# Gate and up projections on one core: four low-part matmuls, then four high-part ones, per four k-blocks

## The chip, the core and the metric

The kernel runs on one core of a Trainium2 chip. The metric is the device time of one execution in microseconds (us); lower is better. Before the change it is 994.61 us, the median of three runs (993.76 to 994.87).

## What is computed

One layer of a decoder: sparse attention, a residual with a layer norm, a SwiGLU feed-forward block, and again a residual with a layer norm. There are 256 tokens of width 2048. The change touches the feed-forward block alone:

```python
D_MODEL = 2048
FFN_HIDDEN = 5632
def _swiglu(x, w_gate, w_up, w_down):
    return (jax.nn.silu(x @ w_gate) * (x @ w_up)) @ w_down
...
x = _layer_norm(DEEPNORM_ALPHA * x + m, ln1_g, ln1_b)
x = _layer_norm(DEEPNORM_ALPHA * x + _swiglu(x, w_gate, w_up, w_down), ln2_g, ln2_b)
```

All arrays are float32.

## The kernel before

**High and low parts.** The matrix engine is fed with fp32r, a reduced form of float32. To keep accuracy each factor is split in two: ScalarE copies a weight block from `raw` to `w_hi` in fp32r (L523), VectorE writes what is left over, `raw - w_hi`, to `w_lo` (L796). Activations are held the same way: `act_t[:, k, 0, :]` is the high part of k-block k (128 of the 2048 model dimensions by 256 tokens), `act_t[:, k, 1, :]` its low part. A product is then high times high, high times low, and low times high.

**Gate and up.** The hidden width of 5632 is cut into 44 column blocks of 128 (`KF`), called tiles. For one tile, gate and up each fill a PSUM bank by summing over the 16 k-blocks (`KD`). Per k-block and bank there are two matmuls. The *high part* (L1247) has the stationary operand `w_hi` and the moving operand `act_t[:, k, :, :]`, 512 columns: both parts of the activation. The *low part* (L1243) has the stationary operand `w_lo` and the moving operand `act_t[:, k, 0, :]`, 256 columns, and adds into the first half of the same bank. Each of the two has a weight load of its own. A tile is 64 matmuls: 2 banks, 16 k-blocks, a high and a low part.

**Slots.** `w_hi` and `w_lo` are rings of four slots. A slot holds eight k-blocks, so a tile takes four slots, j = 0 to 3: gate k 0 to 7, gate k 8 to 15, up the same. `ffn_tile` (L1260) waits in front of each j for VectorE's `lo_done`, calls `pairs` (L1240) for runs of two k, and behind each j raises `pe_used` (or `ffn_full` behind the last), which lets ScalarE overwrite the slot. `pairs` issues low part, low part, high part, high part for two k. For k = 0 it issues the high part first, since that matmul clears the bank. The first tile is written apart (`first_tile`, L1215, its matmuls L1221 and L1223), with 256- and 128-column matmuls for the halves of the tokens. The other 43 tiles go through `ffn_tile`: one call, then a loop of 21 turns with two tiles each.

**Around it.** SyncE issues the loads of the gate and up weights (L356, the DMA at L317), 1 MB per two slots, each waiting for `lo_done` of the block that used its place. While PE works on a tile, ScalarE and VectorE split the weights of the next one and turn the sums of the last one into `hid_t` (L582 to L590, L900 to L908). The order of each engine's program is written out by hand; semaphores join them.

**Other stages named below.** The index-query projection uses the helper `pair` (L1000 to L1004), which alternates a low and a high part per k, again with 256 and 512 columns, and with the high part first at k = 0. The down projection (`product`, L1100) is made of 512-column matmuls alone, three per k-block and token half, with `hid_t` as the stationary operand.

Of the kernel before, what the change touches and what calls it, by code (L numbers as in the profile page):

```python
# [30 lines left out]
P = 128  # L31
# [3 lines left out]
KD = D // P  # L35
# [71 lines left out]
def ring_index(v):  # L107

    x_before = sum(1 for b in X_BLOCKS for h in (0, 1) if 2 * b + h < v)
    return v - x_before  # L110


def layer_kernel(nc, a):
    ctx = ExitStack()
    with ctx:
        def sb(name, shape, dt=F32):
            return ctx.enter_context(nc.sbuf_tensor(name, shape, dt))
# [9 lines left out]
        act_t = sb("act_t", [P, KD, 2, S], F32R)  # L127
# [866 lines left out]
        def _(pe):  # L994
# [16 lines left out]
            for k, t in steps:  # L1011
                v = 2 * IN_BLOCKS[k // 2] + k % 2
                w = ring_index(v) % RING
# [3 lines left out]
                for x_part, w_part in ((0, w_hi), (0, w_lo), (1, w_hi)):  # L1017
                    for b, c0, c1 in spans:
                        last = pe.matmul(acc[:, 2 * t + b, 0:c1 - c0],  # L1019
                                         act_t[:, k, x_part, t * P:(t + 1) * P], w_part[:, w, c0:c1],  # L1020
                                         start=(k == 0 and x_part == 0 and w_part is w_hi),
                                         stop=(k == KD - 1 and x_part == 1))
# [6 lines left out]
            for t in range(TOK):  # L1029
                for n in range(KQ + KV + 1):  # L1030
                    if n == 0:
                        pe.wait_ge(proj_q_done, t + 1)
                    if n == KQ:
                        pe.wait_ge(proj_done, 2 * TOK + t + 1)
                    last = pe.transpose(tp[:, n // 2, (n % 2) * S + t * P:(n % 2) * S + (t + 1) * P],
                                        proj[:, t, n * P:(n + 1) * P], ident[:])
# [24 lines left out]
            for h in range(IDX_HEADS):  # L1061
# [4 lines left out]
                for t, c0, n in ((0, 0, P), (1, P, S)):  # L1066
                    last = pe.matmul(tp[:, h % 4, c0:c0 + n], qidx_t[rows, h // 2, t * P:(t + 1) * P],
                                     kidx_t[rows, 0:n], start=True, stop=True)
# [73 lines left out]
            for s in range(HEADS + 3):  # L1142
                if s < HEADS:
# [4 lines left out]
                    for t, c0, n in ((0, 0, P), (1, P, S)):  # L1148
                        last = pe.matmul(tp[:, s % 2, c0:c0 + n], q_t[:, g % 2, h, t * P:(t + 1) * P],  # L1149
                                         k_t[:, g % 2, h, 0:n], start=True, stop=True)  # L1150
# [5 lines left out]
                if 2 <= s < HEADS + 2:  # L1156
# [4 lines left out]
                    for n in range(KEYS // P):  # L1161
                        last = pe.transpose(tp[:, 2, n * P:(n + 1) * P], prob[:, u % 3, n * P:(n + 1) * P],  # L1162
                                            ident[:])
                    last.then_inc(pt_full, 1)
                if s >= 3:
# [3 lines left out]
                    if u >= 1:  # L1169
# [6 lines left out]
                              stop=True).then_inc(pv_full, 1)  # L1176
# [60 lines left out]
                            turn_in(1, 2 + k // 2)  # L1237
                last.then_inc(ffn_full, 1)

            def pairs(bank, w, e0, k):  # L1240

                def low_part(n):
                    pe.matmul(acc[:, bank, 0:S], w_lo[:, w, e0 + n * P:e0 + (n + 1) * P], act_t[:, k + n, 0, :],  # L1243
                              start=False, stop=False, skip_group_check=True)

                def high_part(n):
                    return pe.matmul(acc[:, bank, :], w_hi[:, w, e0 + n * P:e0 + (n + 1) * P],  # L1247
                                     act_t[:, k + n, :, :], start=(k + n == 0), stop=(k == KD - 2 and n == 0))

                if k == 0:  # L1250
                    high_part(0)
                    low_part(0)
                    low_part(1)
                    return high_part(1)
                low_part(0)
                low_part(1)
                high_part(1)
                return high_part(0)

            def ffn_tile(c, i):  # L1260
                tile = 2 * i + c
                if not (isinstance(i, int) and i == 0):
                    pe.wait_ge(ffn_comb, tile - 1)
                for j in range(4):
                    pe.wait_ge(lo_done, 2 * R_FFN + 4 * tile + j + 1)
                    for n in range(0, 8, 2):
                        k = 8 * (j % 2) + n
                        last = pairs(2 * c + j // 2, j, n * P, k)
                    last.then_inc(*((pe_used, 1) if j < 3 else (ffn_full, 1)))

            first_tile()
            ffn_tile(1, 0)
            with pe.Fori(1, KF // 2) as i:
                ffn_tile(0, i)
                ffn_tile(1, i)
# [79 lines left out]
```

## Time and profile before

| what | value |
|---|---|
| runs, median (lowest to highest) | 994.61 us (993.76 to 994.87) |
| the profiled execution's own time | 994.41 us |
| its span on the core | 992.6 us |
| mean granted TensorE clock | 0.992 of full speed |
| PE (matmul) busy | 962.3 us, 97% of the span |
| PEld (weight load) busy | 826.1 us, 83% |
| VectorE (DVE) busy | 577.9 us, 58% |
| ScalarE (ACT) busy | 522.6 us, 53% |

The profile is of one execution. PE is the matmul side of TensorE and PEld its weight-load side; they overlap. Matmuls are pipelined and the ends in their records are modelled, so two records of one engine can overlap, and what a matmul costs is read from one start to the next. In the timeline, consecutive instructions of the same kind are merged into one row, with the start of the first and a count (x2, x3). The granted clock is the share of full speed (2.4 GHz) that TensorE had; 1.00 is the 2.4 GHz level and 0.50 the 1.2 GHz level.

### The profile page before, as it was taken

What the parts mean: (1) busy time and instruction counts of PE and PEld (TensorE: products, weight loads), DVE (VectorE), ACT (ScalarE), POOL (GpSimd) and SP (SyncE); (2) the same over time, 40 slices, a digit from 0 to 9 for tenths busy, and PEclk for the clock granted to TensorE, in tenths of its full rate; (3) what the DMA queues carried; (4) which work ended last, traced back from release to release, by engine and by line L of the source; (5) the groups of instructions that cost most, each with busy time, mean ns of one, the idle gap of its engine ahead of it and who ended that gap; (6) DMA issues with size and microseconds to landing.
All of it is one profiled execution on the core that took longest, in us unless ns stands there. A gap on an engine that the chain in (4) does not pass through costs nothing.

```text
span 992.6 us, 13665 instructions
## 1 busy us (share of the span) xinstructions
PE 962.3 (97%) x5134; PEld 826.1 (83%) x5134; DVE 577.9 (58%) x787; ACT 522.6 (53%) x720; POOL 41.1 (4%) x40
## 2 busy tenths in 40 slices
PE   6988999999999999999999999999999999999995
PEld 5867888888988888888888888888888888888884
DVE  5469876568655555555555555555555454454555
ACT  5465775354455555666555555666544343343450
POOL 0003650000000000000000000000000000000000
PEclk9979999999999999999999999999999999999998
DMA  8742332566254555555555545555538465565632
GB/s 329 275 146 82 128 128 89 209 248 260 90 207 172 202 175 194 186 185 195 177 203 174 203 173 199 181 187 193 178 123 344 170 207 196 180 213 168 217 122 85
DMA packets 27117, 183.52 MB, mean 185 GB/s; under 512 B 3024, under 2 KB 3024, under 8 KB 7504
## 3 DMA queue, kind: packets, MB, share of 16 engines
q1 hardware_dynamic: 27056, 183.12, 51.9%
q8 instruction: 20, 0.33, 0.1%
q0 software_dynamic: 32, 0.00, 0.0%
q14 instruction: 9, 0.07, 0.0%
HBM read 181.01 MB, written 2.10 MB: 184 GB/s over the span
## 4 chain that ended last, share of the span: by engine, by line
PE 94%; DVE 4%; ACT 1%; issue 1%; DMA 0%; POOL 0%; DVEq 0%; ACTq 0%; POOLq 0%
PE acc L1100 33%; PE acc L1247 32%; PE acc L1243 16%; PE acc L1019 4%; PE acc L1004 1%; PE acc L1088 1%; PE acc L1221 1%; PE tp L1149 1%; PE acc L1003 1%; PE acc L1000 1%; DVE score L716 1%; PE tp L1162 0%; DVE work L746 0%; DVE w_lo L659 0%; DMA raw<-in_x_t 0%
## 5 line engine op out<-in xcount | busy, mean ns | idle before, releaser
L796 DVE TENSOR_TENSOR w_lo<-raw,w_hi 128x1024 fp32r<-128x1024 f32 (+1 forms) x286 | 340.9, 1195 | 330.5 <-ACT w_hi L523 329.5
L523 ACT ACTIVATE w_hi<-raw 128x1024 fp32r<-128x1024 f32 (+1 forms) x278 | 287.7, 1036 | 349.6 <-PE acc L1247 195.8
L1247 PE MATMUL acc<-act_t,w_hi 128*128 128x512 f32 x1376 | 432.6, 396 | 0.0
L1243 PEld LDWEIGHTS acc<-act_t,w_lo 128*128 128x128 f32 x1376 | 258.7, 188 | 57.2
L1243 PE MATMUL acc<-act_t,w_lo 128*128 128x256 f32 x1376 | 271.0, 278 | 0.0
L1247 PEld LDWEIGHTS acc<-act_t,w_hi 128*128 128x128 f32 x1376 | 216.0, 189 | 3.5
L1100 PE MATMUL acc<-w_hi,hid_t 128*128 128x512 f32 x672 | 207.3, 389 | 0.0
L1100 PEld LDWEIGHTS acc<-w_hi,hid_t 128*128 128x128 f32 x672 | 126.1, 188 | 26.1
L1100 PE MATMUL acc<-w_lo,hid_t 128*128 128x512 f32 x336 | 130.8, 389 | 0.0
L1100 PEld LDWEIGHTS acc<-w_lo,hid_t 128*128 128x128 f32 x336 | 63.1, 188 | 13.2
L1100 PE MATMUL acc<-w_hi,o_t 128*128 128x512 f32 x224 | 72.8, 397 | 0.0
L659 DVE TENSOR_TENSOR w_lo<-raw,w_hi 128x1024 fp32r<-128x1024 f32 (+1 forms) x38 | 43.1, 1144 | 18.3 <-ACT w_hi L405 18.2
L405 ACT ACTIVATE w_hi<-raw 128x1024 fp32r<-128x1024 f32 (+1 forms) x42 | 41.6, 1000 | 17.2 <-PE acc L1019 14.7
L1100 PEld LDWEIGHTS acc<-w_hi,o_t 128*128 128x128 f32 x224 | 42.1, 188 | 8.5
L1100 PE MATMUL acc<-w_lo,o_t 128*128 128x512 f32 x112 | 43.6, 390 | 0.0
L1019 PE MATMUL acc<-w_hi,act_t 128*128 128x512 f32 (+1 forms) x128 | 31.3, 366 | 9.8 <-DVE w_lo L659 9.8
L1019 PEld LDWEIGHTS acc<-w_hi,act_t 128*128 128x128 f32 x128 | 22.7, 196 | 12.8 <-DVE w_lo L659 9.8
L900 DVE TENSOR_TENSOR comb<-acc,low 128x512 f32<-128x512 f32 x44 | 30.1, 683 | 1.4 <-ACT low L582 1.4
L989 POOL TENSOR_SCALAR prob<-prob,row_inv 128x128 f32<-128x128 f32 (+1 forms) x24 | 28.8, 1213 | 21.3 <-DVE row_inv L768 21.3
L582 ACT ACTIVATE low<-acc 128x512 f32<-128x512 f32 x44 | 25.5, 580 | 4.9 <-PE acc L1223 4.9
L1004 PE MATMUL acc<-cq_t,w_hi 128*128 128x512 f32 x72 | 27.3, 407 | 0.0
L586 ACT ACT_TABLE_LOAD x21 | 26.9, 1283 | 0.4
(134 smaller groups left out, 756.7 us busy)
## 6 DMA issues: line engine op xcount, KB each, us to landing
raw<-in_w_gu SPq DMA_DIRECT2D x88, 1024.0 KB, 4.8
raw<-in_w_down SPq DMA_DIRECT2D x32, 1024.0 KB, 4.8
raw<-in_w_out SPq DMA_DIRECT2D x16, 1024.0 KB, 4.8
raw<-in_w_down SPq DMA_DIRECT2D x16, 768.0 KB, 4.2
raw<-in_w_in SPq DMA_DIRECT2D x7, 848.0 KB, 6.5
raw<-in_w_uq SPq DMA_DIRECT2D x4, 1024.0 KB, 4.8
raw<-in_w_ukv SPq DMA_DIRECT2D x4, 1024.0 KB, 4.7
ln_rows<-in_ln_rows SPq DMA_DIRECT2D x4, 1024.0 KB, 7.1
```

Of the source, the lines that this page charges most:

```text
L405: act.activation(w_hi[:, w % RING, 0:n], raw[:, r % RING, half * n:(half + 1) * n], ACT.Copy).then_inc(hi_done, 1)
L523: act.activation(w_hi[:, (2 * slot + half) % RING, 0:n], raw[:, slot, first:first + n], ACT.Copy).then_inc(hi_done, 1)
L586: act.activation(sig[:], comb[:, 0, :], ACT.Silu).then_inc(ffn_sig, 1)
L659: dve.tensor_tensor(w_lo[:, w % RING, 0:n], raw[:, r % RING, half * n:(half + 1) * n], w_hi[:, w % RING, 0:n], ALU.subtract).then_inc(lo_d ...
L796: dve.tensor_tensor(w_lo[:, h, 0:n], raw[:, slot, first:first + n], w_hi[:, h, 0:n], ALU.subtract).then_inc(lo_done, 1)
L900: dve.tensor_tensor(comb[:], acc[:, 2 * c:2 * c + 2, 0:S], low[:], ALU.add).then_inc(ffn_comb, 1)
L989: pool.tensor_scalar(prob[:, s % 3, cols], prob[:, s % 3, cols], row_inv[:, (s + 1) % 2, t:t + 1], None, ALU.mult).then_inc(prob_done, 1)
L1004: return pe.matmul(acc[:, bank, :], wh, rhs, start=False, stop=stop)
L1019: last = pe.matmul(acc[:, 2 * t + b, 0:c1 - c0], act_t[:, k, x_part, t * P:(t + 1) * P], w_part[:, w, c0:c1], start=(k == 0 and x_part == ...
L1100: last = pe.matmul(acc[:, bank0 + t, :], lhs[:, k, x, t * P:(t + 1) * P], part[:, w, n * GC:(n + 1) * GC], start=(start and x == 0 and par ...
L1243: pe.matmul(acc[:, bank, 0:S], w_lo[:, w, e0 + n * P:e0 + (n + 1) * P], act_t[:, k + n, 0, :], start=False, stop=False, skip_group_check=True)
L1247: return pe.matmul(acc[:, bank, :], w_hi[:, w, e0 + n * P:e0 + (n + 1) * P], act_t[:, k + n, :, :], start=(k + n == 0), stop=(k == KD - 2 ...
```

## The change

`pairs` becomes `fours`. For four k it issues four low parts, in rising k, and then four high parts, in falling k. For k = 0 the high part of k = 0 still comes first. `ffn_tile` calls it for n = 0 and 4 instead of n = 0, 2, 4, 6. The flag that closes a bank's sum (`stop`) moves with the last high part.

```diff
-            def pairs(bank, w, e0, k):
+            def fours(bank, w, e0, k):
 
                 def low_part(n):
                     pe.matmul(acc[:, bank, 0:S], w_lo[:, w, e0 + n * P:e0 + (n + 1) * P], act_t[:, k + n, 0, :],
...
                 def high_part(n):
                     return pe.matmul(acc[:, bank, :], w_hi[:, w, e0 + n * P:e0 + (n + 1) * P],
-                                     act_t[:, k + n, :, :], start=(k + n == 0), stop=(k == KD - 2 and n == 0))
+                                     act_t[:, k + n, :, :], start=(k + n == 0), stop=(k == KD - 4 and n == 0))
 
                 if k == 0:
                     high_part(0)
-                    low_part(0)
-                    low_part(1)
-                    return high_part(1)
-                low_part(0)
-                low_part(1)
-                high_part(1)
-                return high_part(0)
+                for n in range(4):
+                    low_part(n)
+                for n in (3, 2, 1, 0) if k > 0 else (3, 2, 1):
+                    last = high_part(n)
+                return last
...
-                    for n in range(0, 8, 2):
+                    for n in (0, 4):
                         k = 8 * (j % 2) + n
-                        last = pairs(2 * c + j // 2, j, n * P, k)
+                        last = fours(2 * c + j // 2, j, n * P, k)
```

## Rows read from the trace of the kernel before

**Rows 1.** The page: engines, chain, the two costly matmul groups, loads of gate and up.

```profile
PE 962.3 (97%) x5134; PEld 826.1 (83%) x5134; DVE 577.9 (58%) x787; ACT 522.6 (53%) x720; POOL 41.1 (4%) x40
...
PE 94%; DVE 4%; ACT 1%; issue 1%; DMA 0%; POOL 0%; DVEq 0%; ACTq 0%; POOLq 0%
PE acc L1100 33%; PE acc L1247 32%; PE acc L1243 16%; PE acc L1019 4%; PE acc L1004 1%; PE acc L1088 1%; PE acc L1221 1%; PE tp L1149 1%; PE acc L1003 1%; PE acc L1000 1%; DVE score L716 1%; PE tp L1162 0%; DVE work L746 0%; DVE w_lo L659 0%; DMA raw<-in_x_t 0%
...
L1247 PE MATMUL acc<-act_t,w_hi 128*128 128x512 f32 x1376 | 432.6, 396 | 0.0
...
L1243 PE MATMUL acc<-act_t,w_lo 128*128 128x256 f32 x1376 | 271.0, 278 | 0.0
...
raw<-in_w_gu SPq DMA_DIRECT2D x88, 1024.0 KB, 4.8
```

**Rows 2.** Busy time by stretch, gate and up stage behind its first tile.

```profile
core 0: us, PE busy (x) PEld busy (x) DVE busy (x) ACT busy (x) POOL busy (x), PEclk, DMA share, GB/s
262.80:742.40 479.60, 479.60 (x2753) 418.88 (x2753) 265.42 (x300) 282.94 (x342) 0.00 (x0) 1.00 0.53 185
```

**Rows 3.** Who waited for whom, 263 to 742 us (total, times, longest).

```profile
DVE w_lo L796 <- ACT w_hi L523: 202.7, 171, 2.7
ACT w_hi L523 <- PE acc L1247: 194.2, 130, 1.9
```

**Rows 4.** Timeline of PE: first matmul of `ffn_tile`, first of the down projection.

```profile
262.80 0.45 PE L1247 MATMUL acc<-act_t,w_hi 128*128 128x512 f32 x1
...
742.76 0.39 PE L1100 MATMUL acc<-w_hi,hid_t 128*128 128x512 f32 x1
```

**Rows 5.** Timeline of PE in the stage, 400 to 408 us.

```profile
400.29 0.40 PE L1243 MATMUL acc<-act_t,w_lo 128*128 128x256 f32 x2
400.52 0.63 PE L1247 MATMUL acc<-act_t,w_hi 128*128 128x512 f32 x2
400.99 0.39 PE L1243 MATMUL acc<-act_t,w_lo 128*128 128x256 f32 x2
...
401.92 0.86 PE L1247 MATMUL acc<-act_t,w_hi 128*128 128x512 f32 x3
402.61 0.40 PE L1243 MATMUL acc<-act_t,w_lo 128*128 128x256 f32 x2
```

**Rows 6.** Timeline of PE, index-query projection; an output begins with each row of L1000.

```profile
61.99 0.40 PE L1000 MATMUL acc<-cq_t,w_hi 128*128 128x512 f32 x1
...
63.62 0.28 PE L1001 MATMUL acc<-cq_t,w_lo 128*128 128x256 f32 x1
63.74 0.28 PE L1003 MATMUL acc<-cq_t,w_lo 128*128 128x256 f32 x1
63.87 0.40 PE L1004 MATMUL acc<-cq_t,w_hi 128*128 128x512 f32 x1
...
69.00 0.39 PE L1000 MATMUL acc<-cq_t,w_hi 128*128 128x512 f32 x1
```

**Rows 7.** Timeline of PE, two k per output; first and last of three starts.

```profile
122.68 0.39 PE L1000 MATMUL acc<-ckv_t,w_hi 128*128 128x512 f32 x1
...
124.08 0.39 PE L1000 MATMUL acc<-ckv_t,w_hi 128*128 128x512 f32 x1
```

**Rows 8.** Timeline of PE, down projection; 16 repeats of three matmuls lie between.

```profile
800.35 0.62 PE L1100 MATMUL acc<-w_hi,hid_t 128*128 128x512 f32 x2
...
811.23 0.62 PE L1100 MATMUL acc<-w_hi,hid_t 128*128 128x512 f32 x2
```

**Rows 9.** Timeline of PE in the first tile; five matmuls lie between.

```profile
246.62 0.33 PE L1221 MATMUL acc<-act_t,gu_hi 128*128 128x256 f32 x1
...
247.31 0.33 PE L1221 MATMUL acc<-act_t,gu_hi 128*128 128x256 f32 x1
```

**Rows 10.** Timeline of PE, index-query projection, two microseconds earlier.

```profile
60.59 0.42 PE L1003 MATMUL acc<-cq_t,w_lo 128*128 128x256 f32 x1
60.81 0.63 PE L1004 MATMUL acc<-cq_t,w_hi 128*128 128x512 f32 x1
61.23 0.34 PE L1003 MATMUL acc<-cq_t,w_lo 128*128 128x256 f32 x1
```

**Rows 11.** Busy time by stretch, for the granted clock (third number from the end).

```profile
57.00:61.20 4.20, 3.94 (x12) 3.44 (x13) 3.73 (x6) 2.47 (x4) 0.00 (x0) 0.50 0.02 4
61.99:69.00 7.01, 7.01 (x41) 6.12 (x40) 4.39 (x7) 4.63 (x8) 0.00 (x0) 1.00 0.44 150
```

## The prediction

> **What bounds the kernel now.** I began with the page. TensorE (PE) is busy 97% of the span, and the chain that ended last lies 94% on PE, 32% at L1247 and 16% at L1243, the two lines of the function that changes [rows 1]. "Busy" proves little where matmul records overlap, so the next view was the busy time by stage: in the gate and up stage, from 262.80 us, PE has no idle time in 479.60 us, at a granted clock of 1.00 (the 2.4 GHz level), while ScalarE is busy 282.94 us and VectorE 265.42 us of it [rows 2]. The waits of the stage say the same: ScalarE waited 194.2 us for matmuls of L1247, VectorE 202.7 us for ScalarE, and no row has PE waiting for anybody [rows 3]. So the stage lasts as long as PE's stream of instructions, and the down projection behind it is again PE's own. A nanosecond won per matmul arrives at the end of the kernel whole.
>
> **The unit of account.** Durations are of no use here: a record shows 278 or 396 ns [rows 1], but those overlap. Only the distance from one start to the next counts. One tile (one of 44 column blocks of gate and up) is 64 matmuls, 32 high parts of 512 columns and 32 low parts of 256. From the first start, 262.80 us, to the first start of the down projection, 742.76 us, there are 43 tiles [rows 4]: 479.96 / 43 = 11.16 us each, or 11.16 / 8 = 1.395 us for four k (four low, four high). Inside, two low parts take about 0.23 us and two high parts 0.47 [rows 5]: 0.70 us for two k.
>
> **What the change does.** It removes and adds no instruction: 2752 matmuls, as many weight loads, the same operands, the same waits in front of each j and the same increments behind it. Only the order within four k changes: LL HH LL HH becomes LLLL HHHH. Per four k one switch into a run of low parts goes, and one back. There are 43 × 8 = 344 such runs of four k. The first tile (L1215) and all else stand as they are. The DMAs on SP's queue wait for the splits, the splits for the release behind j, and those come in the same order; the loads land 4.8 us after issue at 1024 KB each [rows 1], two per 11.16 us, so they stay covered even if PE gains a few us over the whole stage. ScalarE and VectorE spend about 6.6 and 6.2 us per tile (282.94 / 43, 265.42 / 43), also covered.
>
> **What a switch costs, first estimate.** The trace has the same matmuls in a third order. The index-query projection (L1000 to L1004) does four k as H L L H L H L H, with the same 128x512 and 128x256 shapes at the same clock [rows 11] and with three runs of low parts instead of two. Five of its outputs follow each other without a wait, from 61.99 to 69.00 us [rows 6]: 7.01 / 5 = 1.402 us for four k. Against 1.395 with two runs, a run more costs 0.007 us; one run fewer should give as much back. A check on the stages themselves: where the same helper does two k as H L L H, with one run per two k as in the stage that changes, an output takes (124.08 − 122.68) / 2 = 0.70 us [rows 7], which is this stage's figure; but two outputs rounded to 0.01 us can't tell 0.698 from 0.701, so it only shows that the projection has no cost of its own. Sum: 344 × 0.007 = 2.4 us.
>
> **Second estimate.** The down projection is nothing but 512-column matmuls, each with a weight load of its own. From 800.35 to 811.23 us are 48 of them [rows 8]: 10.88 / 48 = 0.2267 us each, where a high part in the stage before us costs 0.47 / 2, about 0.233. If the two high parts in the middle of the new run of four reach that pace and the two added low parts cost what they do now, a run of four k gains 2 × 0.0063 = 0.0127 us, and all of them 344 × 0.0127 = 4.4 us. Against this: at 401.92 us three high parts follow each other where one bank ends and the next begins, and they take 402.61 − 401.92 = 0.69 us, 0.23 each [rows 5], between the two paces.
>
> I take 3.0 us, nearer to the first, since its rows mix the same two shapes, and keep 2.4 and 4.4. As to the ends outside: if order is worth nothing, it is 0.
>
> **A low part and its weight load.** A load overlaps the matmul in front of it and cannot be shorter than the pace that loads allow. The first tile shows that pace: there 256- and 128-column matmuls alternate, and from 246.62 to 247.31 us six of them with six loads pass [rows 9], 0.69 / 6 = 0.115 us per load. A low part takes 0.23 / 2 = 0.115 to 0.117 now. So low parts already run at the pace of the loads, and I book nothing gained on them. The Trainium skill ("TensorE: Matmul & The Clock Gate", section "LDWEIGHTS (loading the stationary operand)") puts a load at its columns over 1.2, 107 ns for 128 columns; by its figures that is just what a 256-column matmul streams in, so a run of low parts would have no slack, and the sum would be 0 or a loss. The row agrees that the two are level; whether the third and fourth suffer, no row shows.
>
> **Rivals.**
> - *The order is worth nothing: no change, 994.6 us, 0.30.* Each matmul would cost its columns plus a fixed amount. At the 1.2 GHz level 512 columns take 0.42 us from start to start and 256 take 0.21 (60.81 to 61.23, 60.59 to 60.81 us) [rows 10, 11], a column per cycle and nothing besides; at 2.4 GHz that is 0.2133 and 0.1067. The down projection's 0.2267 is 0.0134 above it. If that is the fixed amount, four k take 4 × 0.2133 + 4 × 0.1067 + 8 × 0.0134 = 1.387 us. The measured 1.395 is 0.008 above, and the alternating order 0.015 above, so a term that grows with the switches seems to be there; but it rests on a single other stage, whose operands and neighbours differ. The Trainium skill, same page, section "Back-to-back issue gap", has just such a rule, columns over 2.4 plus 2.5 ns, blind to order: by it this rival is true, though its constant is far below the rows' 13 ns.
> - *Slower: the third and fourth low part wait for their weights, 998.0 us, 0.13.* Place: L1243, n = 2 and 3. A high part in front leaves about 0.12 us of slack to the load behind it (0.233 less 0.115); the first two low parts of a run may live on that, the next two not. Slots of 0.12 us and more for a low part do occur (63.62 to 63.74, 63.74 to 63.87) [rows 6]. If each added low part cost 0.120 instead of 0.115 and the high parts gained nothing, it would be 2 × 0.005 × 344 = 3.4 us. It decides when an inner low part plus an inner high part come to more than half of what two k take now, 0.349 us. Against it: the first tile holds 0.115 without any slack from 512-column matmuls.
> - *Larger gain, 990.2 us, 0.07.* The down projection's pace for high parts as above, 4.4 us, in full.
> - That the change does not do what it says is hardly possible: nothing sits between the emitted order and PE's order of matmuls, and the timeline shows the order as written.
>
> **How the numbers follow.** The profiled execution took 994.41 us, its span 992.6 and 1.8 around it; the median of the runs is 994.61, so sums go over unchanged. Forecast: 994.6 − 3.0 = 991.6 us, chance 0.50. About 0.2%, 2.0 us, is what a measurement of this kernel can tell from no change; the forecast gives 0.30%, not far beyond it, so a part of its own chance (2.4 us less some spread in the runs) lies close to "same". Faster by over 0.2%: 0.54; within: 0.34; slower by over 0.2%: 0.12. The range begins at 989.6 (a gain of 4.4 and half a us of spread) and ends at 996.0, which takes in no change and about half of the slower rival's price. The forecast case alone spans 990.2 to 992.4.
>
> **What would show it.** Right: starts of PE in the stage come in groups of four 128x256 and four 128x512 rows; from the first start to the first start of the down projection there are 477.0 us instead of 479.96, 11.09 per tile; four high parts take 0.92 us instead of 0.93 to 0.94, four low parts 0.46; the down projection and everything ahead of 262.8 us keep their lengths. Wrong in step one, if four k stay at 1.395 us. Wrong towards slower, if four low parts take 0.47 or more and nothing comes back on the high parts. A new wait of PE for w_lo, or a stage that shrinks while the down projection grows, would contradict the claim that PE's stream alone sets the end.

## The result, and the profile after

| | before | after |
|---|---|---|
| median of 16 runs | 994.51 us (992.94 to 995.07) | 996.52 us (995.27 to 997.46) |
| span of the profiled execution | 992.6 us | 994.6 us |
| mean granted TensorE clock | 0.992 | 0.992 |

The change makes the kernel slower: the ratio is 1.0023 with a 95% interval of 1.0016 to 1.0030, that is 1.6 to 3.0 us. I had forecast 991.6 us, and my range ended at 996.0.

The timeline of PE after the change, at the first matmul of `ffn_tile` and at the first of the down projection (columns as in [rows 4]):

```profile
262.48 0.45 PE L1247 MATMUL acc<-act_t,w_hi 128*128 128x512 f32 x1
262.77 0.64 PE L1243 MATMUL acc<-act_t,w_lo 128*128 128x256 f32 x4
263.25 0.86 PE L1247 MATMUL acc<-act_t,w_hi 128*128 128x512 f32 x3
...
744.70 0.39 PE L1100 MATMUL acc<-w_hi,hid_t 128*128 128x512 f32 x1
```

From start to start that is 482.22 us, against 479.96 in [rows 4]: 2.26 us more. What follows the stage takes 994.6 − 744.70 = 249.9 us, before 992.6 − 742.76 = 249.8, and the stage begins 0.3 us earlier. So the whole loss lies in the 43 tiles. The busy time by stretch and the waits show what it is not:

```profile
262.50:744.00 481.50, 481.50 (x2751) 421.07 (x2750) 265.28 (x300) 283.58 (x342) 0.00 (x0) 1.00 0.52 184
```

```profile
DVE w_lo L796 <- ACT w_hi L523: 202.6, 170, 2.6
ACT w_hi L523 <- PE acc L1247: 193.8, 129, 1.7
```

PE still has no idle time, the clock is still 1.00, and the helpers still wait for PE, as in [rows 2, 3]. No wait was added: PE itself needs longer for the same matmuls. The timeline of a run in the middle of the stage:

```profile
389.15 1.09 PE L1247 MATMUL acc<-act_t,w_hi 128*128 128x512 f32 x4
390.08 0.63 PE L1243 MATMUL acc<-act_t,w_lo 128*128 128x256 f32 x4
390.55 1.32 PE L1247 MATMUL acc<-act_t,w_hi 128*128 128x512 f32 x5
```

Four high parts take 390.08 − 389.15 = 0.93 us, and four low parts 0.47, where two of each took 0.47 and 0.23 in [rows 5]: the sign that I had named for "wrong towards slower". The lows grew and the highs gave little back.

Rows are rounded to 10 ns, so for the rest I took the distances between the starts of PE in the trace, in ns, and averaged them by the place of a matmul in its run. "H" is a high part (512 columns), "L" a low part (256), and the number is its place, from 0:

| | L0 | L1 | L2 | L3 | H0 | H1 | H2 | H3 |
|---|---|---|---|---|---|---|---|---|
| before (runs of two) | 114.6 | 116.3 | | | 233.6 | 233.7 | | |
| after (runs of four) | 115.8 | 118.9 | 119.0 | 119.7 | 233.3 | 233.4 | 232.2 | 228.6 |

A tile took 11,160 ns before, the same in each tile to 1 ns. After, it takes 11,199, 11,219 or 11,222 in turn, on average 11,213. (The first of the 43, behind the tile that is written apart, takes 11,243 ns before and 11,263 after, and is left out of these figures and of the tile times below.) Summed over four k, the four lows went from 461.7 to 473.4 ns, 11.8 more, and the four highs from 933.3 to 928.2, 5.1 less. The net loss of 6.7 ns, 344 times, is the 2.3 us.

### The profile page after: what moved, and what is told of

The parts are those of the page before. It is cut to its first block, busy times and chain, and to the rows that moved or that the text cites. A ratio compares the mean times of both kernels' runs of the same rounds, so it can differ in the third digit from the quotient of the medians.

```text
span 994.6 us, 13665 instructions
## 1 busy us (share of the span) xinstructions
PE 964.2 (97%) x5134; PEld 828.1 (83%) x5134; DVE 578.3 (58%) x787; ACT 523.4 (53%) x720; POOL 41.2 (4%) x40
## 4 chain that ended last, share of the span: by engine, by line
PE 94%; DVE 4%; ACT 1%; issue 1%; DMA 0%; POOL 0%; DVEq 0%; ACTq 0%; POOLq 0%
PE acc L1100 33%; PE acc L1247 32%; PE acc L1243 16%; PE acc L1019 4%; PE acc L1004 1%; PE acc L1088 1%; PE acc L1221 1%; PE tp L1149 1%; PE acc L1003 1%; PE acc L1000 1%; DVE score L716 1%; PE tp L1162 0%; DVE work L746 0%; DVE w_lo L659 0%; DMA raw<-in_x_t 0%
## 5 line engine op out<-in xcount | busy, mean ns | idle before, releaser
L1247 PE MATMUL acc<-act_t,w_hi 128*128 128x512 f32 x1376 | 375.2, 394 | 0.0
L1247 PEld LDWEIGHTS acc<-act_t,w_hi 128*128 128x128 f32 x1376 | 235.4, 188 | 30.8
L1243 PEld LDWEIGHTS acc<-act_t,w_lo 128*128 128x128 f32 x1376 | 210.5, 188 | 29.7
L1243 PE MATMUL acc<-act_t,w_lo 128*128 128x256 f32 x1376 | 218.7, 281 | 0.0
```

## The experiments

In all of them `ffn_tile` calls one function per slot of eight k, which issues the matmuls in the order of a list; the waits and increments stand where they stood. As in the change, k = 0 starts with its high part. The alternating order was run four times and the mirrored one 11 times; each of the others below has a single run, and is judged by its stage and tile times in the trace of that run. Two kernels with the same order and shapes (after the change, and "A PSUM bank of their own" below) have stages equal to 0.01 us.

### Runs of one, runs of eight, highs alone, lows alone

The theories at that point were A, that lows in a run pay for their weight loads (the slower rival of the prediction), and B, that switches cost and the loss comes from elsewhere.

**Alternating.**

```diff
-for n in (0, 4): last = fours(2 * c + j // 2, j, n * P, k)
+order = [(part, n) for n in range(8) for part in ("L", "H")]
```

> Low and high part alternate for each k (runs of one), all work kept. Unit: start to start per four k, and the stage from the first L1247-type start of ffn_tile to the first start of the down projection (before 479.96 us, runs of four 482.22). Theory A, a run of low parts is what costs (the weight load of the next low part has no slack once two lows follow each other): every low has a high in front, so four k cost no more than with runs of two, 1.395 us or less, stage 480 or less. Theory B, switches cost as I predicted and the runs of four lose by something else: 1.402 to 1.410 us per four k as in the index-query projection, stage 482.4 to 485. If both hold, the order of two is the best of the three.

Measured: 999.27 us against 994.76 for the kernel before beside it, ratio 1.0052 (1.0035 to 1.0068); the stage takes 485.59 us and a tile 11,293 ns, 1.412 us per four k. Theory A wanted 1.395 or less, so it does not explain the order of the kernels; theory B's 1.402 to 1.410 was closer, a little low.

**Runs of eight.**

```diff
+order = [("L", n) for n in range(8)] + [("H", n) for n in range(7, -1, -1)]
```

> Eight low parts, then eight high ones. Theory A: each further inner low costs about 0.119 to 0.120 us and an inner high about 0.233, so 8 k take about 2.81 us against 2 x 1.4018 = 2.804 now; stage 483 to 484 us. Theory B (fewer switches are worth 0.007 us each): stage 480 to 481. If inner highs settle at the down projection's 0.2267: below 480.5.

Measured: 994.3 us in a single run; the stage takes 480.52 us and a tile 11,173 ns. So from fours to eights the time falls again: neither a cost per inner low (483 to 484) nor an equal price per switch, which the result of runs of four contradicts. The timeline of PE:

```profile
376.72 1.12 PE L1241 MATMUL acc<-act_t,w_lo 128*128 128x256 f32 x8
377.68 2.23 PE L1245 MATMUL acc<-act_t,w_hi 128*128 128x512 f32 x9
379.74 1.12 PE L1241 MATMUL acc<-act_t,w_lo 128*128 128x256 f32 x8
```

Eight lows in 0.96 us are 0.120 each, and nine highs in 2.06 us are 0.229 each. By place, in ns:

| | 0 | 1 | 2 | 3 | 4 | 5 | 6 | 7 |
|---|---|---|---|---|---|---|---|---|
| L | 113.4 | 119.2 | 120.0 | 120.0 | 120.0 | 120.0 | 120.0 | 120.0 |
| H | 233.3 | 235.8 | 228.3 | 232.5 | 230.8 | 226.7 | 226.7 | 226.7 |

This is the clearest view of the case. Each kind has a steady pace, and after a change from lows to highs it takes five highs to reach it.

**Highs alone** (the low parts are left out, and 12 highs are issued per slot) and **lows alone** (the high parts are left out but the first of a bank, each low is issued three times).

```diff
+order = list(range(8)) + [0, 1, 2, 3]    # highs only
...
+order = list(range(8)) * 3               # lows only
```

> Leaves the low parts out and issues 12 high parts per slot of eight k (the first four twice), to read the pace of a high part among high parts in this stage. If a high part is slowed only by the low parts beside it: 0.2267 us as in the down projection. If by its own operands (act_t moving, w_hi stationary): about 0.232 to 0.233.

> Leaves the high parts out but the first of a bank and issues each low part three times (24 per slot, never the same weights twice in a row), to read the pace of a low part among low parts. Theory A, bound by the weight load at the first tile's pace: 0.112 to 0.115 us. Bound by its columns plus the 13 ns that a matmul of the down projection has over its columns: 0.120 us. The second would make the inner lows of the run of four (0.119 us) the normal price and the lows in runs of two the cheap exception.

Measured: 226.7 ns per high (the stage of highs alone, 467.95 us, holds 2064 of them) and 120.0 per low. The timeline of the kernel with lows alone:

```profile
389.77 5.92 PE L1241 MATMUL acc<-act_t,w_lo 128*128 128x256 f32 x48
395.52 0.40 PE L1245 MATMUL acc<-act_t,w_hi 128*128 128x512 f32 x1
```

48 lows in 5.75 us are 0.120 each. With 213.3 and 106.7 ns for the columns at the 2.4 GHz level, each of the two kinds pays 13.3 ns on top. The low's 120 ns, then, is its normal price, and the 114.6 and 116.3 of the kernel before are the exception. The highs at 233 are the other exception, and the two stand next to each other in the stream.

### Theory C, and a version that beats both kernels

Theory C: a tile costs its columns plus 13.3 ns per matmul, 32 × (226.7 + 120.0) = 11,093 ns, plus a surplus per run of lows with the highs behind it. The surplus of runs of eight is (11,173 − 11,093) / 4 = 20 ns. It holds as well by place: the first five highs are 6.6, 9.1, 1.6, 5.8 and 4.1 ns above the pace, the first two lows 6.6 and 0.8 below, 19.8 in all.

**Mirrored runs of 16.** Where one slot ends with lows, the next begins with them:

```diff
+order = ([("H", n) for n in range(8)] + [("L", n) for n in range(7, -1, -1)] if k0 == 0 else
+         [("L", n) for n in range(8)] + [("H", n) for n in range(7, -1, -1)])
```

> Per bank: eight high parts, eight low ones, then (next slot) eight low, eight high, so runs are of 16 and a tile has two runs of low parts in place of four (runs of eight), eight (fours) or 16 (pairs). Theory C: a matmul costs its columns plus 13.3 ns wherever it stands long enough among its like (a high part 0.2267 us, a low part 0.120), and a run of low parts followed by a run of high ones costs 0.020 us on top, spread over the first five high parts (runs of eight measured 11.173 us per tile against 32 x 0.3467 = 11.093; 0.080 / 4 = 0.020). Then a tile takes 11.093 + 2 x 0.020 = 11.133 us, the stage 43 x 11.133 = 478.8 us (before 479.96), the kernel about 993.4. If the order is worth something only through the number of switches at an equal price (my prediction's theory), fitted to runs of eight and of four, the same sign but it can't be fitted to runs of two. If the cost grows with the length of a run: above 480.5.

Measured: a tile takes 11,133 ns, as worked out, and the stage 478.83 us. The kernel takes 992.65 us against 994.22 for the kernel before beside it, ratio 0.9988 (0.9979 to 0.9997): faster than both kernels, by little. The timeline of PE, where a run of lows and the highs behind it form half a tile (384.40 − 378.83 = 5.57 us):

```profile
378.83 3.82 PE L1245 MATMUL acc<-act_t,w_hi 128*128 128x512 f32 x16
382.49 2.08 PE L1241 MATMUL acc<-act_t,w_lo 128*128 128x256 f32 x16
384.40 3.82 PE L1245 MATMUL acc<-act_t,w_hi 128*128 128x512 f32 x16
```

**Runs of three (3, 3, 2).**

```diff
+order = [(part, n) for run in ((0, 1, 2), (3, 4, 5), (6, 7)) for part in ("L", "H") for n in run]
```

> Runs of three, three and two. Theory C, with the transient cut off at the third high part: summing the deviations from the steady pace by place in the run of eight (highs +6.6, +9.1, +1.6 ns, lows -6.6, -0.8), a cycle of three costs 0.010 us and one of two the 0.004 measured: a tile 11.093 + 8 x 0.010 + 4 x 0.004 = 11.19 us, stage 481.2. If cost falls steadily with fewer switches from pairs to fours it would be below 479.96, which the result of runs of four already speaks against.

Measured: a tile takes 11,200 ns, the stage 481.68 us, the one run 994.75 us. That is 10 ns per tile above the estimate.

The orders side by side. The surplus is what a tile takes over 11,093 ns, and the runs of lows in a tile are counted from the timeline:

| order | tile, ns | surplus, ns | runs of lows | surplus per run |
|---|---|---|---|---|
| alternating | 11,293 | 200 | 30 | 7 |
| two (before) | 11,160 | 67 | 16 | 4 |
| three, three, two | 11,200 | 107 | 12 | 9 |
| four (after) | 11,213 | 120 | 8 | 15 |
| eight | 11,173 | 80 | 4 | 20 |
| 16, mirrored | 11,133 | 40 | 2 | 20 |

The total is the number of runs by their price, and the price is not a constant: from 4 ns for runs of two it grows to 20 for runs of eight, and is the same for 16. From two to four the runs halve and their price rises by a factor of 3.6.

A part of this is that a short run ends before the highs have settled. The rows by place in runs of eight, cut off at the length of the run, give 15.7 ns for four (15 measured) and 9.9 for three, so 112 ns per tile for three, three, two (107 measured). But they give 8.3 for two, where 4.2 was measured, and nothing for one, where it was 6.7. In runs of two the second low took 116.3 ns against 119.2 in runs of eight. So the low price of runs of two, on which the loss of the change rests, is measured and not derived from the long runs; why it is so low stays open.

### What the surplus comes from

**One shape for all.** Order of fours, but the low parts have 512 columns; the sum gets a product that the reference has not.

```diff
-pe.matmul(acc[:, bank, 0:S], w_lo[...], act_t[:, k, 0, :], ...)
+pe.matmul(acc[:, bank, :], w_lo[...], act_t[:, k, :, :], ...)
```

> Order of runs of four, but the low parts are widened to 512 columns (both halves of act_t, so the sum gets a product that the reference hasn't), so that all matmuls have one shape. If the transient comes from the change of shape: 64 matmuls at 0.2267 us, a tile 14.51 us, every start 0.226 to 0.227 after the last. If it comes from the change between w_lo and w_hi: the first highs of a run still stand out by 6 to 9 ns.

Measured: 14,507 ns per tile and 226.7 per matmul throughout (64 × 226.7 = 14,509). The timeline of PE:

```profile
389.08 1.07 PE L1245 MATMUL acc<-act_t,w_hi 128*128 128x512 f32 x4
389.98 1.07 PE L1241 MATMUL acc<-act_t,w_lo 128*128 128x512 f32 x4
390.89 1.07 PE L1245 MATMUL acc<-act_t,w_hi 128*128 128x512 f32 x4
```

Four take 0.90 or 0.91 us, whether low or high. The surplus is gone, with the weights still switching between `w_hi` and `w_lo`: it belongs to the change of shape, that is, of the number of columns.

**A PSUM bank of their own.** Order of fours; the low parts sum into a bank that nothing reads, and are missing from the result.

```diff
-pe.matmul(acc[:, bank, 0:S], w_lo[...], act_t[:, k, 0, :], start=False, ...)
+pe.matmul(tp[:, bank, 0:S], w_lo[...], act_t[:, k, 0, :], start=(k == 0), ...)
```

> Order of runs of four, but the low parts sum into a PSUM bank of their own (and stay out of the result), shapes unchanged. If the extra time of lows and first highs comes from adding to the same PSUM columns again after only 256 of them: the first high parts fall to 0.2267 and a tile towards 11.09 us. If the shape alone is behind it: 11.20 to 11.22 us as in the changed kernel, place by place.

Measured: the stage takes 482.22 us, the same as after the change to 0.01 us, and so do the tiles (11,199 to 11,222). Adding to the same columns again has no part in it.

**Other widths of the low part, runs of eight.** Lows of 128 columns (the second half of the tokens lacks its low part), of 384 and of 320 (the sum gets half, or a quarter, of a product too much).

```diff
-acc[:, bank, 0:S], ..., act_t[:, k, 0, :]
+acc[:, bank, 0:128], ..., the first 128 columns of act_t[:, k, :, :]    # also 384, 320
```

> Runs of eight, the low parts cut to 128 columns (the second half of the tokens lacks its low part). Tells what sets the 0.120 us of a low part of 256 columns in a long run. If a matmul is its columns plus 13.3 ns and weight loads can go faster than that: 0.0667 us per low. If the weight load sets a floor: a low stays at the pace of loads, 0.107 to 0.120 us (0.115 in the first tile). At exactly 0.120 the load is what sets the 256-column low too.

> Runs of eight, the low parts widened to 384 columns, so that they cover their weight loads with 0.05 us to spare (the sum gets half a product too much). Low parts: 160 + 13.3 = 0.1733 us by either theory. If the 0.020 us that the high parts behind a run of lows cost comes from weight loads running at their pace in the run, it goes, and 8 k take 8 x (0.1733 + 0.2267) = 3.200 us, every high at 0.2267. If it comes from the change of shape as such: the first five highs stand out again, 3.21 to 3.22 us.

> The same with 320 columns, 25 ns above the steady low of 256. Low parts 133.3 + 13.3 = 0.1467 us. Cause in the loads: highs at 0.2267 from the first on, 8 k in 2.987 us. Cause in the shape: a surplus of the same size as with 256 or 384 columns.

Measured, in three kernels. Lows of 128 columns:

```profile
377.04 1.00 PE L1242 MATMUL acc<-act_t,w_lo 128*128 128x128 f32 x8
377.88 1.85 PE L1246 MATMUL acc<-act_t,w_hi 128*128 128x512 f32 x7
```

Lows of 384 columns:

```profile
377.19 1.55 PE L1242 MATMUL acc<-act_t,w_lo 128*128 128x384 f32 x8
378.58 2.24 PE L1246 MATMUL acc<-act_t,w_hi 128*128 128x512 f32 x9
380.66 1.57 PE L1242 MATMUL acc<-act_t,w_lo 128*128 128x384 f32 x8
```

Lows of 320 columns:

```profile
378.22 1.33 PE L1242 MATMUL acc<-act_t,w_lo 128*128 128x320 f32 x8
379.39 1.77 PE L1246 MATMUL acc<-act_t,w_hi 128*128 128x512 f32 x7
```

At 128 columns a low inside a run takes 111.8 ns on average, although its columns plus 13.3 would be 66.7. The columns can't account for it, and I read it as the pace of weight loads. A low of 256 columns at 120.0 stands 8 ns above this floor, so it is not bound by its load. At 384 columns a low takes 0.174 us, far above the floor, and yet the surplus is there and larger: a tile takes 13,000 ns against 32 × (173.3 + 226.7) = 12,800, 50 ns per run, in lows (up to 179.1 at place 3) and highs (up to 235.8) alike. At 320 columns a tile takes 12,027 against 32 × (146.7 + 226.7) = 11,947, 20 ns per run, and the highs settle place by place as with 256. So lows that are held at the pace of their loads are not the cause. Each of these kernels still has one load per matmul, so that the loads have some part in how a mixed stream settles is not excluded, and why 384 columns cost more than 320 and 256 is open. The mechanism inside TensorE that makes a stream need several matmuls to settle after a change of column count was not found: these runs fix where it acts and how much it takes, not what it is.

## Why the prediction was wrong

- *What bounds the kernel, and the unit of account:* right. The whole difference lies in PE's starts within the stage and arrives whole at the end (2.26 us in the stage, 2.0 in the span and in the medians).
- *First estimate, 2.4 us gained:* this is the step that failed: "one run fewer should give as much back". The slope between three runs per four k and two was real, and in this stage steeper than in the projection: alternating lost 5.63 us of the stage (485.59 − 479.96), 9.5 ns per run more, against the 7 that I had read. But I had two points and drew a line through them. The price of a run depends on its length, 4 ns at two and 15 at four, and fewer runs at a higher price came out dearer: (120 − 67) × 43 = 2.3 us.
- *Second estimate, 4.4 us gained:* its two conditions failed. "If the two high parts in the middle of the new run of four reach that pace": the pace of 226.7 is real in this stage too, but reached only at the sixth high of a run; in runs of four the middle ones took 233.4 and 232.2. "And the two added low parts cost what they do now": now is 115, and the added ones cost 119.0 and 119.7, since 120.0 is the normal price. Of the 12.7 ns booked for four k the highs gave back 5.1, and the lows, booked at nothing, took 11.8. The three highs that [rows 5] had shown at 0.23 each, and that I placed "between the two paces", were a warning.
- *A low part and its weight load:* wrong reading. "So low parts already run at the pace of the loads": the floor is 112 ns, lows alone settle at 120.0 above it, and the first tile's 115 and the lows' 115 agreed by accident. The term that I booked at nothing on this ground is the larger part of what the second estimate missed. The rule of the Trainium skill ("TensorE: Matmul & The Clock Gate", section "LDWEIGHTS (loading the stationary operand)"), 107 ns for 128 columns, lies 5 ns below the floor measured with 128-column lows. It pointed to no gain or a loss, and a loss there was, but not by that way: the lows are not bound by their loads.
- *The order is worth nothing:* wrong, but its arithmetic held something. The fixed 0.0134 us is the true price of both shapes, and its 1.387 us for four k is exactly the steady pace, 4 × 346.7. (The 256 columns that I put at 0.21 us are 0.22 by [rows 10]; the trace has 213 to 214 ns, so nothing follows from it.) The rule of the Trainium skill ("TensorE: Matmul & The Clock Gate", section "Back-to-back issue gap"), columns over 2.4 plus 2.5 ns, has the right form for a stream of one shape, with 13.3 ns here in place of 2.5. I had left out that the section gives it for isolated matmuls; for streams of a weight load and a matmul it states about 131 ns per matmul of 512 columns. The 226.7 ns measured here contradict that.
- *The slower rival:* right in the outcome and in the point from which it decides. It needed an inner low and an inner high to come to more than 349 ns together; they came to 119.0 + 232.8 = 351.8. Its 0.120 us for an added low was close to the measured 119.0 and 119.7, but by luck: its mechanism, lows that wait for their weights, fell with the lows of 128 columns, which ran at 112 ns. Its price, 3.4 us, was half too high against 2.3, since it let the highs gain nothing. I had given it 0.13.

## What to carry to other kernels

When a stream of matmuls mixes two column counts, time the steady pace of each alone and the surplus of a switch, before regrouping: the surplus per run grew here from runs of two to runs of eight and then stayed, so that very long runs and runs of two were the good orders, and runs of three, of four and of one the bad ones. Two points of such a curve say nothing about the third. Where a boundary can be mirrored, so that the next block starts with the kind that the last one ended with, half the switches go at no cost: here 40 ns per tile against runs of eight, and 0.12% of the kernel against runs of two.

## What the runs showed of the hardware that I had not expected

- Each matmul pays 13.3 ns over its columns at the 2.4 GHz level in a steady stream (226.7 ns for 512 columns, 120.0 for 256), while at the 1.2 GHz level of [rows 10, 11] the starts lie 213 to 214 and 426 to 427 ns apart, a column per cycle and nothing over it, although 256 and 512 columns are mixed there too.
- After a change from 256 to 512 columns, between long runs, the stream takes five matmuls to settle, 20 ns in all. It is regular to the nanosecond: tiles of equal length in the kernel before, and a pattern that repeats every three tiles in the changed one, though its loop has two tiles.
- The three lengths of a tile in the changed kernel (11,199, 11,219, 11,222 ns) suggest that something is carried over from one tile to the next, since the program of each tile is the same; what it is, no run shows.
- Inside runs of 128-column matmuls with a weight load each, a matmul takes 112 ns.
